# A decoder trunk with expert retrieval on one core: TensorE reports every fourth summed tile instead of every one

## The reference, cut to what matters

```python
def chunk(xc):                                   # 128 tokens at a time
    q = (xc @ wq).reshape(T, PEER_HEADS, 2, PEER_HALF)
    ...                                          # top 16 of 128 x 128 keys in each of 8 heads
    gate = jax.nn.softmax(best_s, axis=-1)
    u_sel = jnp.take(u, idx, axis=0)             # 128 rows of 1024 for each token
    act = jax.nn.gelu(jnp.einsum('thkd,td->thk', u_sel, xc), approximate=False)
    v_sel = jnp.take(v, idx, axis=0)             # and 128 more
    return jnp.einsum('thk,thkd->td', gate * act, v_sel)
```

## Time and profile before

| | |
|---|---|
| median of 3 runs | 1805.06 us (1803.39 to 1805.64) |
| span of the profiled execution, first to last instruction | 1795.7 us |
| median less that span | 9.4 us |
| TensorE busy | 1525.6 us, 85% |
| VectorE busy | 1027.0 us, 57% |
| GpSimd busy | 1101.3 us, 61% |
| ScalarE busy | 387.9 us, 22% |
| moved by DMA | 687.11 MB, mean 383 GB/s |
| mean granted TensorE clock | 0.968 of 2.4 GHz |

### The profile page before, as it was taken

One profiled execution on the slowest core, in us unless ns is written; L12 is line 12 of the kernel. 1 busy time (PEld: TensorE's weight loads), 2 busy tenths in 40 slices (PEclk: granted clock), 3 DMA queues, 4 the chain that ended last, 5 costly groups with the idle time before them and its releaser, 6 DMA issues.

```text
span 1795.7 us, 13519 instructions
## 1 busy us (share of the span) xinstructions
PE 1525.6 (85%) x3952; PEld 672.4 (37%) x3952; DVE 1027.0 (57%) x2479; ACT 387.9 (22%) x965; POOL 1101.3 (61%) x1131
## 2 busy tenths in 40 slices
PE   4998879989988888999997768999989877767777
PEld 3755434443332333444442223444344322222222
DVE  6566854676566562444457775436446876544442
ACT  2222132221111140141312132133222221111110
POOL 4221576766665774656756775656656777766664
PEclk9999989989999999999999989999989999999999
DMA  9998899999999999999999999999999999999997
GB/s 375 399 388 285 285 336 395 393 409 399 404 404 406 406 409 389 399 403 407 404 402 408 410 367 367 403 401 409 394 407 407 366 391 340 392 365 370 365 375 275
DMA packets 214653, 687.11 MB, mean 383 GB/s; under 512 B 20883, under 2 KB 21557, under 8 KB 214582
## 3 DMA queue, kind: packets, MB, share of 16 engines
q0 software_dynamic: 158976, 578.88, 82.9%
q1 hardware_dynamic: 54544, 105.98, 15.7%
q10 hardware_dynamic: 1062, 1.40, 0.2%
HBM read 685.14 MB, written 1.05 MB: 382 GB/s over the span
## 4 chain that ended last, share of the span: by engine, by line
PE 40%; DMA 22%; POOL 17%; issue 9%; DVE 8%; another core or an unknown queue 3%; ACT 1%; DVEq 0%; POOLq 0%
PE pair L1010 20%; PE pair L180 13%; DMA net_u<-in_peer_u,net_cols 12%; POOL net_v L581 8%; POOL net_u L581 8%; DMA net_v<-in_peer_v,net_cols 4%; DVE net_u L1778 4%; DMA net_w<-in_b_w_qo 3%; PE pair L203 2%; PE pair L196 2%; DMA net_w<-in_kv_w 1%; DMA net_v<-in_ada_w 1%; PE pair L613 1%; PE pair L618 1%
## 5 line engine op out<-in xcount | busy, mean ns | idle before, releaser
L1010 PE MATMUL pair<-net_v,net_diags 128*128 128x512 f32 x2048 | 976.5, 612 | 161.4 <-DMA net_v<-in_peer_v,net_cols 91.6
L581 POOL DMA_INDIRECT net_v<-in_peer_v,net_cols x512 | 521.7, 1019 | 331.0 <-PE pair L1010 151.3
L581 POOL DMA_INDIRECT net_u<-in_peer_u,net_cols x512 | 517.4, 1011 | 224.8 <-issue 139.8
L1010 PEld LDWEIGHTS pair<-net_v,net_diags 128*128 128x128 f32 x2048 | 373.0, 192 | 709.0 <-issue 492.2
L1778 DVE SCALAR_TENSOR_TENSOR net_u<-net_u,pair 128x1024 f32<-128x1024 f32 x320 | 386.9, 1218 | 275.2 <-DMA net_u<-in_peer_u,net_cols 185.6
L180 PE MATMUL pair<-net_w,net_work 128*128 128x512 f32 x624 | 294.4, 611 | 22.5 <-DMA net_w<-in_b_w_qo 14.3
L1354 ACT ACTIVATE net_diags<-ident,net_cols 128x128 f32<-128x128 f32 x512 | 171.1, 392 | 657.8 <-DVE net_cols L1450 354.5
L1778 DVE SCALAR_TENSOR_TENSOR net_u<-net_u,net_x_tok 128x1024 f32<-128x1024 f32 x192 | 233.2, 1220 | 98.0 <-DMA net_u<-in_peer_u,net_cols 71.0
L180 PEld LDWEIGHTS pair<-net_w,net_work 128*128 128x128 f32 x624 | 119.7, 196 | 168.5 <-issue 160.7
L1450 DVE TENSOR_TENSOR net_cols<-net_cols,net_gate 128x4 f32<-128x4 f32 (+1 forms) x124 | 19.9, 161 | 129.8 <-ACT net_cols L1347 109.5
L225 POOL DMA_DIRECT2D net_u<-in_ada_w x46 | 24.8, 541 | 80.5 <-DVE net_sc L237 21.1
(11 more groups left out here) (243 smaller groups left out, 977.6 us busy)
## 6 DMA issues: line engine op xcount, KB each, us to landing
net_w<-in_peer_wq SPq DMA_DIRECT2D x12, 2048.0 KB
net_u<-in_ada_w POOLq DMA_DIRECT2D x46, 512.0 KB, 9.3
net_w<-in_ada_w SPq DMA_DIRECT2D x8, 2048.0 KB
net_w<-in_kv_w SPq DMA_DIRECT2D x8, 2048.0 KB
net_w<-in_b_w_qo SPq DMA_DIRECT2D x8, 2048.0 KB
net_v<-in_ada_w POOLq DMA_DIRECT2D x18, 512.0 KB, 12.6
net_u<-in_kv_ada_w POOLq DMA_DIRECT2D x16, 512.0 KB, 6.6
net_u<-in_peer_u,net_cols POOLq DMA_INDIRECT x512
```

Source lines behind the costliest of these rows:

```text
L581: eng.indirect_dma_start(slot, None, rows, bass.IndirectOffsetOnAxis(ap=idx[:, i, k:k + 1], axis=0)).then_inc(landed, 16)
L1010: mm = eng.matmul(acc[q % 2][:, at], diag[n % DIAGS][:, :], vb[n % V_SLOTS][:, at], start=(k == 0), stop=(k == SEL - 1))
```

## The change

TensorE raises `summed` after the last matmul of tiles 3, 7, 11 and so on, and no longer after each. Whoever waits for tile n now waits for `n // 4 + 1` signals, that is for the last tile of n's group of four: tile n itself or one up to three tiles later. Three places wait: GpSimd before it gathers v tile m, for tile m - 10; ScalarE before it writes diagonal n, for tile n - 16; VectorE in `add_ffn`, for tile 127 of a group of 128, which is the last of its four. On each engine the instructions, their number and their order are as before.

```diff
+    SUM_EVERY = 4
+
+    def summed_through(n):
+        return n // SUM_EVERY + 1
...
                     if m >= V_SLOTS:
-                        eng.wait_ge(summed, m - V_SLOTS + 1)
+                        eng.wait_ge(summed, summed_through(m - V_SLOTS))
                     gather(v_rows, m, vb[m % V_SLOTS], v_in[m % V_SLOTS])
...
-                mm.then_inc(summed, 1)
+                if n % SUM_EVERY == SUM_EVERY - 1:
+                    mm.then_inc(summed, 1)
                 behind.upto(n)
...
                     if n >= DIAGS:
-                        eng.wait_ge(summed, n - DIAGS + 1)
+                        eng.wait_ge(summed, summed_through(n - DIAGS))
                     eng.activation(diag[n % DIAGS][:, :], chip.ident[:, :], ACT.Copy, scale=w[:, n:n + 1]
...
-                eng.wait_ge(summed, SEL * (q + 1))
+                eng.wait_ge(summed, summed_through(SEL * (q + 1) - 1))
```

## The result

The changed kernel takes 1826.23 us (median of 4 runs, 1820.3 to 1834.43), the kernel before 1805.35 us beside it (1803.39 to 1810.4). The ratio is 1.0115, with a 95% interval from 1.0078 to 1.0153: slower by some 21 us, where 1812 was forecast and 1803 to 1824 was the range. The sign was right and the size a third of it. Ratios leave out two executions, one of e4 and one of e18, that ran in a slower state.

The account below looks back on a forecast made before the run. The prediction saw TensorE and DMA both full, DMA full alone, or GpSimd's issue limiting the tail. Terms 1 + 2 + 4 + 4 - 5 + 1 = 7 us on the 1795.7 span gave 1802.7, plus 9.4 to the median, 1812; range 1803 to 1824.

Parts of the forecast that it names:

- What bounds the kernel, and who waits: TensorE and DMA both full, DMA full alone, or GpSimd's issue in the tail; v's gathers waited 151.3 us for TensorE.
- same: Rival: weight loads cover every DMA idle stretch, or the second chain's gain pays; 1802 to 1808 us, chance 0.27.
- faster: Rival: weight loads come sooner (1792 us) or fewer signals save TensorE time (1799 us); chance 0.10.
- root came late: Rival: late small roots stop TensorE's transposes; about 1820 us for one or two, 1832 for four; chance 0.13.
- Signals, ScalarE, VectorE at nothing: Fewer signals save TensorE 0 us, ScalarE's later diagonals cost 0, VectorE's wait is unchanged.
- The first chain, 4 us: Near 700 us GpSimd is silent from 685.2 to 708.3; 4 us of DMA idle, bounds 0 and 8.
- The second chain, 4 - 5 + 1: Near 1110 us: 4 us of DMA idle, 5 back from a shorter weight wait, 1 for a later root.
- the gain of 5: After the second chain, TensorE's weight wait of 6.01 us shrinks as gathers are held; 5 us back.
- The roots, 0: First chain's root, through VectorE, is ready at 717.5, wanted by TensorE's transposes at 720.14; 2.6 us to spare, cost 0.
- 400 to 482 us ... I take 2, bounds 0 and 6: v62 waits for tile 55, GpSimd is silent 10.4 us instead of 4.5; a weight load covers most, 2 us.
- it falls idle only where a wait was long already: Where TensorE holds GpSimd, the DMA loses time only at holds that were long before the change.
- in the steady part ... the DMA does not fall idle: Where TensorE holds GpSimd, the queue fills and drains once a group, beside weight loads, without DMA idle.

Follow-up runs that it names:

- e4: Kernel before with GpSimd's wait made coarse (by fours) only for the group of tiles 48 to 51; ratio 1.0021 (0.9993 to 1.0048).
- e18: Changed kernel with TensorE's three column sums between tiles 48 and 51 each made five times over; ratio 1.0333 to the kernel before.
- e8: Kernel before with GpSimd's wait in fours only for tiles 384 to 511, the tail; ratio 0.9993 (0.9975 to 1.0011).
- e2: Kernel before with its 512 signals, only ScalarE's wait for a free diagonal made in fours; ratio 1.0009 (0.9991 to 1.0027).
- e3: Kernel before with one more signal a tile, to a semaphore on which nobody waits; ratio 1.0017 (0.9998 to 1.0036).
- e6: Kernel before with GpSimd's wait in fours only for tiles 128 to 255, the first chain; ratio 1.0056 (1.0035 to 1.0077).
- e7: Kernel before with GpSimd's wait in fours only for tiles 256 to 383; ratio 1.004 (1.0011 to 1.0068).
- e1: Kernel before with its 512 signals, only GpSimd's wait for a slot of v made in fours; ratio 1.0147 (1.0123 to 1.017).
- e5: Kernel before with GpSimd's wait in fours only for tiles 0 to 127; ratio 1.0072 (1.0045 to 1.0099).
- e9: Changed kernel with a signal every two tiles (256 signals), all three engines counting in twos; ratio 0.9996 to the kernel before, on the second kind of chip.
- e13: The changed kernel itself, run again on the second kind of chip; ratio 1.0048 (1.0034 to 1.0062) to the kernel before.

## Why the prediction was right, and where it was wrong

*What bounds the kernel, and who waits.* Right. The stretches with TensorE and DMA both full lose; the pure gather stretches (438 to 684 us, 0.0) and the tail (e8; v waited 8.7 us for TensorE after 1400 us, against 10.0) don't.

*The rivals.* None of them came: the interval from 1.0078 up leaves out both "same" and "faster", and no root came late (below).

*Signals, ScalarE, VectorE at nothing.* Right for ScalarE (e2) and, by the chain's 429 ns, for the signals (e3 leaves 0 to 6 us by its ratio). VectorE's wait was not changed by itself; its tile is the last of a group either way.

*The first chain, 4 us.* Right by the traces: 5.0 on the first kind, 3.9 on the second. GpSimd stood 15.65 us in one piece until 717.58, where I had forecast over 20, and from 710 to 720 us the DMA moved 152 GB/s. But e6, the whole second quarter, cost 1.0056, 10 us. Against before its trace loses 14.5 us: 5.9 from 260 to 400 MB, 4.7 in the 20 MB from 388 us, where its waits are fine, and 5.0 after 1032 us, where nearly all are. So what of its ratio is chance stays open.

*The second chain, 4 - 5 + 1.* The net was right on the first kind, -0.3 to +0.4 in a spread of 7 us among the fine traces, and +3.2 on the second. Its parts were not: GpSimd's longest hold there was 11.8 us in after, as long as before, and not 20 or more, and the gain of 5 was too large. The two weight waits did shrink. What were 7.23 and 6.01 us are in TensorE's timeline of after, one and the other:

```profile
702.71 2.90 PE L180 MATMUL pair<-net_w,net_work 128*128 128x512 f32 x3 [5.09 <-DMA net_w<-in_b_w_qo]
...
1122.15 2.38 PE L180 MATMUL pair<-net_w,net_work 128*128 128x512 f32 x5 [3.56 <-DMA net_w<-in_b_w_qo]
```

That is 2.1 and 2.5 us less.

*The roots, 0.* Right. They come later: VectorE waited 63.8 us for them in place of 34.4. But everything else of the chain comes later too: in after VectorE's product behind the root ends at 726.5 and the transposes start at 729.2, so 2.7 us were to spare, where the forecast had 2.6. From 700 to 800 and from 1100 to 1200 us TensorE waited for weight loads alone.

*The term that failed: "400 to 482 us ... I take 2, bounds 0 and 6".* It is 7.3 us on chips of the first kind (4.8 at equal stops) and 0.0 on those of the second. I looked for the longest wait of before (v 62) and made it longer; in after v 62 was held 4.3 us, and not 10.4. The gather that costs is v 58, which waited for nothing before, because the tiles 49 to 51 that it now waits for lie across the column sums, where the earlier trace rows don't reach and where TensorE stands without a releaser: 6.9 us in before's one trace, 13.8 in after's. The rule "it falls idle only where a wait was long already" is what failed. A coarse wait turns a stop of the producer inside a group into a hold of all its slots, if the stop ends later than the consumer's turn comes. At equal stops the 4.8 is within the bounds 0 and 6, more than twice the 2, and paid at another gather for another reason. And a bound taken from one trace of TensorE's times was no bound: that place takes 49.6 to 54.5 us in kernels with unchanged waits there.

*The term that was missing, and the larger one: 1238 to 1441 us, 8.6 us*, or 7.2 by e7's ratio for the whole quarter. I had written off what follows the second chain with "in the steady part ... the DMA does not fall idle". It isn't so on the first kind of chip. The size rests on three coarse traces against a spread of 8 us among the fine ones; on the second kind of chip it is absent, though holds of 5.4 us are there as well. That TensorE's stops make the difference here too is argued from e1's one hold, not shown.

*What is shown and what isn't.* Shown: GpSimd's coarse wait is the cause; three quarters carry it; near 400 us the coarse wait costs 4.8 us at equal stops of TensorE and nothing without a stop; the same kernel, after, loses 1.0048 where no engine stands without a releaser, and 1.0115 or, by its wait alone, 1.0147 where they do; a stop put in by hand makes the coarse wait dearer at its place (one trace each). Argued only: that these stalls are the whole of the difference between the kinds of chip. Open: what the stalls are, and whether coarse waits lengthen them. At the column sums they were 13.8, 11.1 and 13.2 us in after, e1 and e5 and 5.8 to 11.2 in the seven others of the first kind; e4, coarse at this very place, had 5.8, so it may be chance. e5's profiled run, 1802.4 us, is 10 us under its median, so its trace shows the least of its losses. Twos, and fours with 11 slots, were not run on a chip of the first kind.

No version beat the kernel before. The nearest is e9: half the signals, no loss that can be measured on the second kind (0.9996 and 1.0001).

## What to carry to other kernels

Before a release is made coarse, write down for every group what else the producer does between its first and its last member, and what the queue's consumer needs in that time: the cost is not in the mean distance but in the groups that straddle other work, also where no wait stood before. Where the slack is thin, one slot more (here 11 in place of 10, with 8 diagonals) or a group of two instead of four takes most of the cost away (1.0012 and 1.0001 beside 1.0048 on the same chip; neither ran on a chip of the first kind). And a sum made from one trace holds for that chip: take the spread of each stretch over several unchanged kernels as the bound of a term, not a row of one.

## What the runs showed of the hardware

Two kinds of chip ran the same program some 2.5% apart: before took 1799 to 1807 us wherever the first kind ran (at least three chips), 1759 us on the two of the second. Each chip ran in one sitting, so whether this belongs to the chip or to its state at that hour is open. In the tail the first kind moves 359 GB/s, the second, in e13,

```profile
1395.00:1762.00 367.00, 282.43 (x576) 98.53 (x576) 210.02 (x496) 59.53 (x179) 261.56 (x267) 1.00 0.99 392
```

and beside that stand GpSimd's waits after 1400 us, in after (total, times, longest; "remote" means that the profile names no instruction of this core as the releaser):

```profile
POOL net_v L586 <- remote: 35.1, 7, 5.9
```

Seven stops of up to 5.9 us before a gather of v, the last five some 45 us apart, with no slot to wait for. Before has five there, 21.3 us in all, and e13 has none. On TensorE the stops of over 1 us without a releaser add up to 13 to 47 us a run on the first kind, after 300 us. The Trainium skill (Runtime: NRT & Kernel Launch, "Instruction fetch mechanics") has each engine fetch its instructions in blocks of 16 KiB by a DMA queue of its own, mostly hidden. It was my guess for the stops, but the traces don't bear it out: the 16 KB transfers on the instruction queue took 1.09 us in the median in after and in e13 alike, and of the 34 stops of TensorE and GpSimd in after only three have one beside them. What the stops are stays open.
